# Hybrid pool/SSD decoder step on one core: RMS-norm factors by token rows, opening and tail reordered, third tile's low parts between additions

## The reference

```python
def rmsnorm(x, g):
    y = x * lax.rsqrt(jnp.mean(x * x, axis=-1, keepdims=True) + EPS)
    return y * g
def swiglu(h, w_gate, w_up, w_down):
    return (jax.nn.silu(h @ w_gate) * (h @ w_up)) @ w_down
x = x + 0.5 * swiglu(rmsnorm(x, g_ffn1), w1_gate, w1_up, w1_down)      # 2816 hidden
mix, ... = token_mix(rmsnorm(x, g_mix), ...)   # causal pooling + Mamba-2 SSD, w_in, conv, w_out
x = x + mix
x = x + cross_attn(rmsnorm(x, g_xq), k_mem, v_mem, w_xq, w_xo)          # 4 heads, 256 memory rows
x = x + 0.5 * swiglu(rmsnorm(x, g_ffn2), w2_gate, w2_up, w2_down)
y = rmsnorm(x, g_final)
```

## Time and profile before

| what | before |
|---|---|
| median of 3 runs | 2381.19 us |
| the profiled execution | 2378.9 us |
| its span, first to last instruction | 2377.2 us |
| PE matmul busy | 2326.0 us (98%), 14994 instructions |
| DVE busy | 1241.7 us (52%) |
| ACT busy | 593.3 us (25%) |
| mean granted TensorE clock | 0.991 |

### The profile page before, as it was taken

One profiled execution on the slowest core, in us unless ns is written; L12 is line 12 of the kernel. 1 busy time (PEld: TensorE's weight loads), 2 busy tenths in 40 slices (PEclk: granted clock), 3 DMA queues, 4 the chain that ended last, 5 costly groups with the idle time before them and its releaser, 6 DMA issues.

```text
span 2377.2 us, 37042 instructions
## 1 busy us (share of the span) xinstructions
PE 2326.0 (98%) x14994; PEld 2244.9 (94%) x14994; DVE 1241.7 (52%) x2301; ACT 593.3 (25%) x1020; POOL 58.6 (2%) x100
## 2 busy tenths in 40 slices
PE   7999999999999899999999999999999999999998
PEld 7999999999999899985789988999999999999998
DVE  5544444444445775454867635266444444444445
ACT  6111111111112332234623124141111111111112
POOL 0000000000000000012210000000000000000000
PEclk8999999999999999998999999999999999999999
DMA  4111111111111321056523424311111111111111
GB/s 147 36 54 35 53 35 53 53 41 47 35 53 41 111 55 53 30 155 213 198 78 101 152 90 151 117 54 36 54 35 53 53 52 36 42 46 50 39 36 74
DMA packets 185419, 169.21 MB, mean 71 GB/s; under 512 B 6659, under 2 KB 165137, under 8 KB 185065
## 3 DMA queue, kind: packets, MB, share of 16 engines
q1 hardware_dynamic: 185329, 167.94, 22.6%
HBM read 147.98 MB, written 20.04 MB: 71 GB/s over the span
## 4 chain that ended last, share of the span: by engine, by line
PE 60%; DVE 2%; ACT 1%; issue 1%; DVEq 0%; ACTq 0%
PE bank L2237 17%; PE bank L2238 17%; PE bank L2239 17%; PE bank L2813 1%; PE bank L2825 1%; PE bank L2717 1%; PE bank L2713 1%; PE bank L2845 1%; PE bank L2923 0%; PE bank L2722 0%; PE bank L2834 0%; PE bank L2867 0%; PE bank L2733 0%; PE bank L2657 0%; PE bank L2855 0%
## 5 line engine op out<-in xcount | busy, mean ns | idle before, releaser
L2237 PE MATMUL bank<-h_hi,w_hi 128*128 128x352 f32 x3120 | 1012.6, 325 | 5.2 <-DVE pre L1524 2.2
L2239 PE MATMUL bank<-h_hi,w_lo 128*128 128x352 f32 x3120 | 1001.1, 321 | 0.0
L2238 PE MATMUL bank<-h_lo,w_hi 128*128 128x352 f32 x3120 | 1001.0, 321 | 0.0
L2237 PEld LDWEIGHTS bank<-h_hi,w_hi 128*128 128x128 f32 x3120 | 586.4, 188 | 8.2 <-DVE pre L1524 2.8
L2238 PEld LDWEIGHTS bank<-h_lo,w_hi 128*128 128x128 f32 x3120 | 587.7, 188 | 0.8
L2239 PEld LDWEIGHTS bank<-h_hi,w_lo 128*128 128x128 f32 x3120 | 586.0, 188 | 0.0
L1401 DVE SCALAR_TENSOR_TENSOR x<-bank,x 128x352 f32<-128x352 f32 x528 | 275.8, 523 | 191.4 <-PE bank L2239 191.1
L2237 PE MATMUL bank<-mid_hi,w_hi 128*128 128x352 f32 x1056 | 342.4, 324 | 8.1 <-DVE x L1401 8.1
L2238 PE MATMUL bank<-mid_lo,w_hi 128*128 128x352 f32 x1056 | 339.2, 321 | 0.0
L2239 PE MATMUL bank<-mid_hi,w_lo 128*128 128x352 f32 x1056 | 338.9, 321 | 0.0
L1316 DVE TENSOR_TENSOR w_lo<-w_raw,w_hi 128x1024 fp32r<-128x1024 f32 x190 | 229.3, 1235 | 50.3 <-ACT w_hi L859 48.4
(11 more groups left out here) (334 smaller groups left out, 1474.9 us busy)
## 6 DMA issues: line engine op xcount, KB each, us to landing
w_raw<-in_w_gate_dram SPq DMA_DIRECT2D x44, 512.0 KB, 3.8
w_raw<-in_w_up_dram SPq DMA_DIRECT2D x44, 512.0 KB, 4.5
w_raw<-in_w_down_dram SPq DMA_DIRECT2D x44, 512.0 KB, 4.1
w_raw<-in_w_in_dram SPq DMA_DIRECT2D x18, 512.0 KB, 4.8
x_spill<-x SPq DMA_DIRECT2D x6, 1408.0 KB, 6.2
kring<-in_cache_mem_k_dram SPq DMA_DIRECT2D x8, 1024.0 KB, 5.0
vring<-in_cache_mem_v_dram SPq DMA_DIRECT2D x8, 1024.0 KB, 5.0
dec<-acs_row SPq DMA_DIRECT2D x8, 768.0 KB, 6.1
```

What stands on the lines that cost most here:

```text
L2237: eng.matmul(out, a_hi, b_hi, start=first, stop=False)
L2238: eng.matmul(out, a_hi, b_lo, start=False, stop=False)
L2239: return eng.matmul(out, a_lo, b_hi, start=False, stop=last)
```

## The change

1. **Opening.** The parameter rows are loaded after the first token row, ahead of the other two and of the weights; PE transposes them after `x_turn(0)`. `x_turn(3)` moves behind the first 24 matmuls. ACT takes `x_evac(6)` and one square ahead of its first Silu turn, and `x_evac(7)` ahead of its second; it splits half of the high parts of tile 2 off behind turn 2. DVE takes `x_evac(6)` ahead of the split of weights 4 and 5, and the eight low parts of tile 2 go from one block ahead of turn 3 to between the additions of the first `ffn_down` (`low=0`).
2. **Norms inside.** `norm_stat` becomes three one-column matmuls with the sums of squares as the stationary operand: the sum of a token lands on its own partition. The Newton iteration runs on `[128, 3]`; three diagonals and a new `norm_spread` (three matmuls of 128 columns) and a copy (`norm_factors`) bring the factors to `rb`. Nine times. The spreads stand in PE's list in `ffn_down` of tile 2 behind block 4 (1, 0), in w_in behind the first product of (pair 0, n 2) and of (pair 1, n 0) for (1, 1) and (1, 2), in `project_all` for (3, 0) to (3, 2) and (4, 0), and in `ffn_first` behind turn 1 (4, 1) and behind the first block of `ffn_down` of tile 0 (4, 2).
3. **State rows** are loaded ahead of weights 4 and 5 of w_in; on DVE the split of weights 2 and 3 of w_in moves behind the first four evictions.
4. **Tail.** `y_turn` is cut into halves; the rows of t = 5 and 6 begin when the first four blocks are added, the last reduction runs ahead of three halves and two rows, and DVE sums a block one step later, behind the next addition.

The diff, cut to its core:

```diff
 # SP
-            for t in range(3):
-                xload(t)
-            ffn_unit(U_F1, "w1", 0, 0)
-            ffn_unit(U_F1, "w1", 0, 1)
+            xload(0)
...
+            xload(1)
+            xload(2)
+            ffn_unit(U_F1, "w1", 0, 0)
+            ffn_unit(U_F1, "w1", 0, 1)
             xload(3)
...
-            for k in range(4, 6):
-                unit(U_IN + k, ...)
             eng.wait_ge(s_spill, 48)
             eng.wait_ge(n_lo, split_at(1, 2, 7))
             eng.wait_ge(n_sq, 3)
             eng.dma_start(convrow[:, :], ...)
             eng.dma_start(poolrow[:, :], ...)
+            for k in range(4, 6):
+                unit(U_IN + k, ...)
 # ACT
-            for t in (3, 4, 5):
-                r_square(t)
+            x_evac(6)
+            r_square(3)
             ffn_turn(0, 0, 0)
+            r_square(4)
+            r_square(5)
             hi_unit(U_F1, 4, 0)
             hi_unit(U_F1, 5, 0)
-            x_evac(6)
+            x_evac(7)
             ffn_turn(0, 0, 1)
             r_square(6)
-            x_evac(7)
             r_square(7)
...
-            for k in range(KT):
+            for k in range(3):
                 norm_hi(2, k, x, G1)
-            for t in (2, 3):
-                ffn_turn(0, 0, t)
+            ffn_turn(0, 0, 2)
+            for k in range(3, KT):
+                norm_hi(2, k, x, G1)
+            ffn_turn(0, 0, 3)
 # DVE
             def norm_rs(v, n):
-                eng.tensor_scalar(ms, bank[6][:, 0:TN], 1.0 / D, EPS, ALU.mult, ALU.add).then_inc(n_ms, 1)
-                newton(ms, rb[:, cols(n)], s)
+                eng.tensor_scalar(nrm[:, 0, sl], bank[6][:, 384:387], 1.0 / D, EPS, ALU.mult, ALU.add).then_inc(n_ms, 1)
+                newton(nrm[:, 0, sl], nrm[:, 1, sl], nrm[:, 2, sl])
+                eng.wait_ge(x_bc, spread_at(v, n))
+                for c_ in range(3):
+                    eng.tensor_scalar(diag[:, c_ * P:(c_ + 1) * P], ident[:, :], nrm[:, 1, 3 * n + c_:3 * n + c_ + 1], None,
+                                      ALU.mult).then_inc(x_dg, 1)
+
+            def norm_factors(v, n):
+                eng.wait_ge(x_bc, spread_at(v, n) + 1)
+                link(eng.tensor_copy(rb[:, cols(n)], bank[6][:, 0:TN]))
+                eng.sem_inc(x_rb, 1)
                 eng.sem_inc(n_rs, 1)
...
             def ffn_tail(u0, f, i, low=None):
                 for m in range(KT):
+                    if low is not None:
+                        eng.wait_ge(tr_dve, 9)
+                        norm_lo(low, 2, m, x, G1)
                     ffn_add(f, i, 0, m)
...
             norm_rs(1, 0)
             for m in range(KT):
                 ffn_add(0, last, 2, m)
+            norm_factors(1, 0)
             for k in range(KT):
                 norm_lo(1, 1, k, x, GMIX)
+            norm_sum(1, 1)
             for k in range(KT):
                 norm_lo(1, 2, k, x, GMIX)
-            norm_sum(1, 1)
-            w_split(U_F1 + 8, last)
-            w_split(U_F1 + 9, last)
...
             norm_rs(1, 1)
+            norm_sum(1, 2)
+            norm_factors(1, 1)
             evict_in(0, 1, 0)
             evict_in(0, 1, 1)
-            norm_sum(1, 2)
+            w_split(U_F1 + 8, last)
+            w_split(U_F1 + 9, last)
             norm_rs(1, 2)
+            norm_factors(1, 2)
 # DVE, tail (m now runs to KT)
+                if m < KT:
+                    ffn_add(1, last, 2, m)
-                elif m > 1:
+                elif m > 2:   # sums block m - 1
 # PE
             def norm_stat(v, n):
-                eng.matmul(bank[6][:, 0:TN], ones[:, :], sq[:, 0, :], start=True, stop=True).then_inc(n_st, 1)
+                eng.wait_ge(x_rb, spread_at(v, n))
+                for c_, a in enumerate((0, P, TN - P)):
+                    mm = eng.matmul(bank[6][:, 384 + c_:385 + c_], sq[:, 0, a:a + P], ones[:, 0:1], start=True, stop=True)
+                mm.then_inc(n_st, 1)
+
+            def norm_spread(v, n):
+                eng.wait_ge(x_dg, 3 * spread_at(v, n) + 3)
+                for c_, a in enumerate((0, P, TN - P)):
+                    mm = eng.matmul(bank[6][:, a:a + P], ones[:, :], diag[:, c_ * P:(c_ + 1) * P], start=True, stop=True)
+                mm.then_inc(x_bc, 1)
...
-                ffn_down(u0, f, i, 2)
+                ffn_down(u0, f, i, 2, between=lambda m: norm_spread(v, 0) if m == 4 else None)
...
+                        if (pair, n, mm) in ((0, 2, 0), (1, 0, 0)):
+                            norm_spread(1, 1 + pair)
...
+                            if group == 0 and n and (first, four) == (3, 0):
+                                norm_spread(3, n)
+                            if last is not None and group == 1 and n == 2 and four == 3:
+                                norm_spread(last, 0)
...
             ffn_down(U_F2, 1, last, 2, between=y_between)
-            for t in (5, 6):
-                y_turn(t)
+            y_half(5, 0)
+            y_half(6, 0)
+            y_half(5, 1)
             eng.wait_ge(n_sum, N_END + 2 + KT - 1)
             y_stat(1)
+            y_half(6, 1)
             for t in (7, 8):
                 y_turn(t)
```

## The result

| | before | changed |
|---|---|---|
| median (6 runs each) | 2380.67 us | 2364.01 us |
| lowest to highest | 2378.52 to 2382.19 | 2362.14 to 2366.85 |
| profiled execution (span) | 2378.9 (2377.2) | 2363.87 (2362.2) |

The ratio is 0.9928 (95% interval 0.9912 to 0.9943): 0.7% faster, 16.7 us between the medians and 15.0 between the profiled executions. The forecast was 2369.0 with a range from 2364 to 2375; it named the right side and was 5 us too cautious, at the very edge of its range.

What follows compares the result with a forecast made beforehand. PE bounds the loops, so gains lie in seam waits and half clock: 5.9 + 6.3 - 2.6 + 0 + 2.7 = 12.3 us off 2378.9 gives 2366.6; plus 2.3, about 2369.0, range 2364 to 2375.

Steps and rivals of the forecast that it cites:

- The forecast's case: Whole kernel: PE's waits and half clock at the seams shrink or go, time 2369.0 us; chance 0.62.
- (a) to (d): Rivals: clock stays halved, 0.13; opening gives little, 0.13; slower, PE waits for diagonals, 0.04; seams' waits move on, 0.08.
- The step from the sum to the median: Whole kernel: 2.3 us added to 2366.6, since the median shown stood that far above the profiled execution.
- price of a norm on PE: Each of nine norms: spread 0.67 us plus statistic 0.2 dearer, 0.9 us more on PE.
- Opening, front: Opening: earlier parameter rows less the exposed `x_turn(3)`, net gain 0.4 us; a new 0.5 us wait in `x_turn(5)`.
- Opening, back: Later opening: gains 5.1 wait, 1.8 half clock, 1.2 additions; loses 1.4 at `x_turn(8)`, 0.7 at the spread.
- Mixer: Seam into the mixer: shorter waits and full clock gain 6.3 us, bounds 3.5 and 7.5.
- PE's path: Mixer seam, low end: PE's own work gives 4.6 us plus what is left of two eviction waits of 2.2.
- DVE's pace: Mixer seam, high end: DVE sets the pace behind spread (1, 2), and its shorter norms give 7 us.
- Attention and second FFN: Attention seam loses 2.6 us, three norms at 0.9; second FFN seam 0, its 2.2 us wait offset by spreads and statistics.
- Tail: End of kernel: the 1.9 us wait goes and one more half moves behind the statistic, gain 2.7 us.
- Rival (a): Opening and mixer seam: the clock stays halved behind remaining waits of 1.5 and 1.2 us, 2373 to 2375; chance 0.13.

Runs made afterwards that it cites:

- e1: The changed kernel as it is, timed again beside the experiments: median 2364.09 us.
- e7: Changed kernel, but ACT takes its first square and third weight split before `x_evac(3)`, and `x_evac(4)` before the third square: median 2363.20 us.
- e8: Changed kernel with the three attention norms alone back in their old, wide form: median 2362.39 us.
- e13: Changed kernel with the third norm's eight low parts again in front of DVE's turn 3, additions following one another: median 2368.92 us.
- e11: Changed kernel with every norm's spread done twice, three more matmuls each of nine times: median 2371.09 us.
- e5: Changed kernel with state rows again after the two weights and DVE's two weight splits ahead of its first evictions: median 2363.77 us.
- e9: Changed kernel with three more wide DVE copies behind `norm_rs(1, 0)`, lengthening the mixer seam's wait to 2.3 us: median 2366.93 us.
- e17: Changed kernel with eight and 26 idle PE transposes in the opening, ahead of the first FFN block: median 2363.79 us.
- e2: Changed kernel with the whole opening of the first FFN put back, norms and tail as changed: median 2371.35 us.
- e10: Changed kernel with seven more wide DVE copies behind `norm_rs(1, 0)`, mixer seam's wait 3.8 us: median 2370.16 us.
- e12: Changed kernel with the ten parameter rows issued by ACT's queue, token rows 0 to 2 and two weights heading SP's: median 2366.59 us.
- e14: Changed kernel with eight and ten idle PE transposes in the opening: median 2363.19 us.
- e16: Changed kernel with the edits of e7 and e8 plus idle PE transposes in the opening: median 2361.58 us.

## Why the prediction was wrong, step by step

The forecast's case came true and (a) to (d) did not, but the time came out 5.0 us lower than the forecast. Two steps failed most. The step from the sum to the median added 2.3 us that are not a property of the kernel. And the term "price of a norm on PE", 0.9 us, was too high: it measured 0.65, which is 2.3 us over nine norms. In the opening the front part was mis-sized the other way (0.4 - 0.5 forecast, -1.33 measured), and its working left out the landing of the first weight. The sum was 2.7 us too small against the profiled execution.

- **From the sum to the median** (2.2 of the 5 us). I added the 2.3 us by which the medians of before stood above its profiled execution. That execution was a quick one: before's medians beside the experiments were 2379.6 to 2381.8, 1 to 3 above it, while the changed kernel's profiled execution, 2363.87, is its median. An offset of one execution is not a property of the kernel; it belonged in the range, not in the sum. Nor is 16.7 itself sharp: beside e1 the difference of the medians was 15.6.
- **Opening, front** (-1.2). I gave it 0.4 - 0.5 = -0.1; at tile 5 PE is 1.33 behind. The 0.4 itself is a slip: 1.2 gained less 1.0 for the exposed turn is 0.2. The parameter rows landed at 6.0, better than the 6.8 I had. But the second token row landed at 8.7, ACT's copies ended at 12.2, not 11.4, and the first FFN matmul came at 15.2, not 14.3. The first weight, now issued behind the ten rows, landed at 12.0 where it had landed at 9.7: even with the copies done at 11.4 its split could not have begun then, and the forecast had no term for that. The turn of tile 3 cost its 1.0 as said, but I charged it to PE alone: ACT's copy of it is first in a list with three squares, two splits and `x_evac(4)`, and these came 2 us later (e7 shows 1.2 of it). And the clock rose at 20.8, 1.1 later than before, so the early start was spent at half clock, 0.29 us a matmul. The forecast's 1.2 had it rise at the same moment. This last part is one execution's and not the change's: where the clock rose at 17.8 (e8, with the same front), PE was 0.1 ahead of before at tile 5, and over the ten traces with this front and ACT order it is between 1.4 behind and 0.1 ahead.
- **Opening, back.** The 5.1 wait and its clock: forecast 6.9, from -1.40 to 6.02 measured 7.4. `x_turn(8)`: forecast a wait of 1.4, measured 1.6; I had `x_evac(7)` at 43.9 and it ended its queue at 44.3. Spread 0.7, measured 0.8. Additions 1.2, measured 1.4 (e13 the same at that place). All about right.
- **Norm on PE** (the largest error in the sum). The spread is 0.67 as forecast (e11). The statistic is not 0.2 dearer. Two steps and the new one take 0.99 us, so it costs 0.67 and not 0.8; the wide one takes 0.91 five times, 1.17 and 1.25 (the other two of the nine have a wait in them), 1.0 on average. The earlier trace rows was one of the cheapest of its kind; against it the new one is 0.08 dearer. So a norm costs some 0.65 and not 0.9, nine of them 2.3 us less; in attention, undone alone, three cost 1.6, or 0.54 each (e8). The six passes took 0.59 us, 0.1 each. The Trainium skill, "TensorE: Matmul & The Clock Gate", section "Wait — 56ns, not 53.3ns?", says that small matmuls never start less than about 25 ns apart; six at that distance would be 0.15 in all. The trace keeps to that bound but does not come near it: the passes took four times as long, and the row of eight in 0.88 that I had taken instead came close.
- **Mixer** (+0.7). 3.5 of wait and 2.2 of clock came as forecast (4.81 to 9.87, with one spread paid), the 1.5 too. I took a value between PE's path (4.6 and something) and DVE's pace (7); e11 says PE's path, which made more than I thought, through the statistics (wide ones of 1.25 and, with the 1.5 wait, 2.67 fell away where the new one takes 0.99 and 0.90) and 0.6 less of waiting at the evictions. State rows and splits: nothing, as said (e5).
- **Attention and second FFN** (+0.9 and +0.8): the same price, three norms each. At (4, 1) the diagonals were 0.3 late (0.4 forecast). In the second FFN another 0.4 came where the spread (4, 0) stands: the profile of before has an idle 1.1 us there on PE (at 1591.2), which is gone with the spread in its place. What it waited for, its profile doesn't say, and no term of the forecast had it.
- **Tail** (+0.3): 3.0 against 2.7, the last turns without a wait. Two stretches that no edit touches gave another 1.1, 0.4 at 1045 to 1130 and 0.7 at 1330 to 1560; in e1 they gave 0.2 and 0, so most of it is luck of the execution.
- **Rival (a)** got 0.13. Its other side is now measured, in the mixer: at 1.2 us the clock stayed (e1), at 2.3 it didn't (e9). The choice was right for the mixer, with a little over 1 us to e9; for `x_turn(8)`, at 1.6, it was luck of the execution (e8 and e17 lost it).

## What to carry to other kernels

A wait on TensorE of some 2 us or more can have a second price behind it, 1.7 us of half clock here. It came behind 4 of 19 waits of 1.5 to 2.2 us at the seams and behind every longer one there, but behind 11 of 19 of the 2.44 us elsewhere. So bringing a 4.7 us wait to 1.2 is worth 5.7, and shortening it to 2.3 would have been worth 2.6 less (e9, one execution). When a tile's turn is moved later on one engine, look at what is queued behind its copy on the next: an in-order list that begins with it stands still. A norm by token rows pays where DVE's length is on the path (mixer, second FFN); where nothing waits for it (attention) it costs 0.5 to 0.6 us a norm for nothing. And a sum taken from one profiled execution gives the time of that execution; how far it stood from its median says nothing of where the next kernel will stand.

## What I had not expected

**A stretch that no edit touches moves the time by up to 10 us.** Between 1045 and 1130 us, where PE waits three times for ACT and DVE, each execution has its own pattern of half clock. Windows of the changed kernel, of e5 and of e13, whose edit lies at 50 us:

```profile
1040.00:1100.00 60.00, 54.92 (x306) 36.72 (x305) 26.87 (x43) 18.70 (x26) 13.10 (x9) 0.97 0.65 199
1100.00:1130.00 30.00, 27.35 (x176) 16.08 (x174) 24.63 (x33) 27.76 (x75) 6.79 (x5) 0.72 0.83 267
```

```profile
1040.00:1100.00 60.00, 53.75 (x306) 35.21 (x304) 26.93 (x43) 19.08 (x26) 13.14 (x10) 1.00 0.68 201
1100.00:1130.00 30.00, 27.88 (x193) 17.13 (x192) 23.98 (x35) 28.04 (x75) 7.12 (x6) 0.77 0.86 279
```

```profile
1040.00:1100.00 60.00, 54.88 (x253) 36.23 (x252) 24.93 (x39) 15.34 (x20) 13.12 (x10) 0.80 0.54 166
1100.00:1140.00 40.00, 38.23 (x223) 22.12 (x223) 25.37 (x40) 29.46 (x74) 8.53 (x6) 0.74 0.80 250
```

The changed kernel spent 20.5 us at half clock here, e5 13.7 (PE 1.2 us earlier at 1130, against e1), e8 27.3 (2.9 later), e13 44.4 (10.3 later; its other runs took 2365.9 to 2369.3 against the profiled 2376.1). Against e1, by the look-up, e2, e10, e11, e12, e14 and e16 lost 1.2, 3.7, 2.8, 1.9, 2.0 and 2.0 there. This can make medians of kernels whose seams differ by 1 us differ by 3, and is why the experiments were read by place and not by total. What decides the pattern stays open: I didn't try a kernel that changes the waits in that stretch. In the changed kernel its three waits make 7.7 us, and 20.5 us at half clock cost, as an estimate, at most another 10.2: more than any one seam of this change gave.
